# Attention with ScalarE's exponentials two units ahead, and the mLSTM state's decay on ScalarE: one core of a Trainium2

## What is computed

```python
s = jnp.einsum('bhtd,bhsd->bhts', qb, kb) * d_w
num = (jnp.einsum('bhts,bhse->bhte', s, vb)
       + inter_w[..., None] * jnp.einsum('bhtd,bhde->bhte', qb, c_mat))
...
h = num / jnp.maximum(jnp.abs(den), jnp.exp(-m_t))[..., None]
...
c_new = decay[..., None, None] * c_mat + jnp.einsum('bhsd,bhse->bhde', kb * w_s[..., None], vb)
```

```python
idx_score = jnp.where(admissible[None], idx_score.astype(jnp.float32), -jnp.inf)
_, sel = lax.top_k(idx_score, k_sel)
...
logits = jnp.einsum('bqgrd,bqkgd->bqgrk', qb, ks).astype(jnp.float32) * scale
p = jax.nn.softmax(logits, axis=-1).astype(v.dtype)
return jnp.einsum('bqgrk,bqkgd->bqgrd', p, vs)
```

## Time and profile before

| | |
|---|---|
| median of 3 runs | 2377.69 us (2368.26 to 2377.85) |
| the profiled execution, its own time | 2379.91 us |
| its span in the trace | 2377.9 us |
| mLSTM stage | 406.7 to 515.07 us |
| attention stage | 515.07 to 697.7 us |
| PE / DVE / ACT / POOL busy | 93% / 75% / 57% / 24% of the span |

### The profile page before, as it was taken

One profiled execution on the slowest core, in us unless ns is written; L12 is line 12 of the kernel. 1 busy time (PEld: TensorE's weight loads), 2 busy tenths in 40 slices (PEclk: granted clock), 3 DMA queues, 4 the chain that ended last, 5 costly groups with the idle time before them and its releaser, 6 DMA issues.

```text
span 2377.9 us, 41523 instructions
## 1 busy us (share of the span) xinstructions
PE 2202.8 (93%) x15519; PEld 1781.8 (75%) x15519; DVE 1793.9 (75%) x2040; ACT 1357.2 (57%) x1513; POOL 565.2 (24%) x466
## 2 busy tenths in 40 slices
PE   6899999859999579999999999999999999999994
PEld 5677887747887467787787787777777778778773
DVE  3699999933423578788788788788778877877886
ACT  4542224754643256666666666667667667667665
POOL 1017785863000011111111111111111211112110
PEclk8779999965999789999999999999999999999997
DMA  5011221020013268799899899899889889889897
GB/s 144 14 45 36 54 52 55 18 81 23 1 30 133 77 241 320 271 339 317 285 333 330 282 328 325 296 325 319 302 307 340 302 302 336 311 296 341 311 376 259
DMA packets 253533, 526.46 MB, mean 221 GB/s; under 512 B 32984, under 2 KB 59736, under 8 KB 253116
## 3 DMA queue, kind: packets, MB, share of 16 engines
q1 hardware_dynamic: 240204, 483.27, 56.5%
q0 software_dynamic: 13264, 42.34, 7.4%
HBM read 490.96 MB, written 35.91 MB: 222 GB/s over the span
## 4 chain that ended last, share of the span: by engine, by line
PE 70%; DMA 10%; DVE 7%; issue 4%; POOL 4%; ACT 3%; SPq 1%; DVEq 0%; ACTq 0%; POOLq 0%
PE ps L1757 13%; PE ps L1759 12%; PE ps L1758 12%; DMA e_raw<-in_w_gate_up_dram 9%; PE ps L1764 8%; PE ps L1425 5%; PE ps L1426 5%; PE ps L1427 5%; PE ps L1630 2%; PE ps L1640 2%; DVE e_wlo L2260 2%; PE ps L1580 2%; PE ps L1769 1%; PE ps L1500 1%; ACT a_p L1231 1%
## 5 line engine op out<-in xcount | busy, mean ns | idle before, releaser
L1308 ACT ACTIVATE e_whi<-e_raw 128x2048 fp32r<-128x2048 f32 x411 | 785.9, 1917 | 423.4 <-PE ps L1759 317.0
L2260 DVE TENSOR_TENSOR e_wlo<-e_raw,e_whi 128x2048 fp32r<-128x2048 f32 x410 | 926.9, 2285 | 68.8 <-ACT e_whi L1308 66.9
L1757 PE MATMUL ps<-e_whi,xh 128*128 128x512 f32 x1088 | 434.5, 399 | 0.0
L1758 PE MATMUL ps<-e_whi,xl 128*128 128x512 f32 x1088 | 424.3, 390 | 0.0
L1759 PE MATMUL ps<-e_wlo,xh 128*128 128x512 f32 x1088 | 424.1, 390 | 0.0
L941 POOL DMA_INDIRECT x_d<-ym,scur x34 | 69.6, 2048 | 867.3 <-ACT ym L1341 846.7
L1757 PEld LDWEIGHTS ps<-e_whi,xh 128*128 128x128 f32 x1088 | 204.2, 188 | 52.6 <-issue 12.7
L1759 PEld LDWEIGHTS ps<-e_wlo,xh 128*128 128x128 f32 x1088 | 204.2, 188 | 44.0
L1757 PE MATMUL ps<-e_whi,ath 128*128 128x512 f32 x544 | 222.3, 409 | 13.6 <-DVE atl L2288 13.6
L1758 PEld LDWEIGHTS ps<-e_whi,xl 128*128 128x128 f32 x1088 | 204.4, 188 | 39.3
L1759 PE MATMUL ps<-e_wlo,ath 128*128 128x512 f32 x544 | 213.8, 393 | 0.0
(11 more groups left out here) (353 smaller groups left out, 3404.1 us busy)
## 6 DMA issues: line engine op xcount, KB each, us to landing
e_raw<-in_w_gate_up_dram SPq DMA_DIRECT2D x275, 1024.0 KB, 6.5
e_raw<-in_w_down_dram SPq DMA_DIRECT2D x136, 1024.0 KB, 11.5
w_raw<-in_w_in_dram SPq DMA_DIRECT2D x20, 512.0 KB, 3.8
xt<-in_x_dram SPq DMA_DIRECT2D x8, 512.0 KB, 6.2
wo_raw<-in_w_out_dram SPq DMA_DIRECT2D x8, 512.0 KB, 7.4
xr<-in_x_dram SPq DMA_DIRECT2D x8, 512.0 KB, 4.2
x_d<-x SPq DMA_DIRECT2D x8, 512.0 KB, 2.6
h_d<-h SPq DMA_DIRECT2D x8, 512.0 KB, 2.9
```

The costliest lines, as they stand in the source:

```text
L1308: nc.scalar.activation(e_whi[:, m % HRING, :], e_raw[:, m % RING, :], ACT.Copy).then_inc(s.e_hi, 1)
L1757: nc.tensor.matmul(dst, a_hi, slot_hi, start=False, stop=False, skip_group_check=True)
L1758: nc.tensor.matmul(dst, a_lo, slot_hi, start=False, stop=False, skip_group_check=True)
L2260: nc.vector.tensor_tensor(e_wlo[:, m % HRING, :], e_raw[:, m % RING, :], e_whi[:, m % HRING, :].bitcast(F32), ALU.subtract).then_inc(s.e_l ...
```

## The change

ScalarE takes over the decay of the state: four ACTIVATE copies with a scale, from `state` to `state`, behind the four copies into `m_in` of the same chunk, with a new semaphore `a_dec`. GpSimd's four multiplications go; its sum now waits for `a_dec`. The waits for `p_in` and `g_st` go with them. In the attention, ScalarE runs `exp(0)` and `exp(1)` first and then, behind each copy `pt_out(u)`, `exp(u + 2)` in place of `exp(u + 1)`; `q_hi_of` and the other copies stand where they stood in the loop. PE's and VectorE's lists are the same, and so are all buffers.

```diff
+        self.a_dec = sem("a_dec")
...
             def m_state(c):
                 gp.wait_ge(s.a_up, c + 1)
-                gp.wait_ge(s.p_in, c + 1)
-                gp.wait_ge(s.g_st, c + 1)
-                for h in range(MH):
-                    m1(nc.gpsimd.tensor_scalar(state[:, h, :], state[:, h, :], decay[:, h, c:c + 1], 1.0, ALU.mult, ALU.mult))
-                m1.done()
+                gp.wait_ge(s.a_dec, c + 1)
                 nc.gpsimd.tensor_tensor(state[:], state[:], m_up[:], ALU.add).then_inc(s.g_st, 1)
...
                         m = nc.scalar.activation(m_in[:, h, :], ps[:, b, o_:o_ + MD + 1], ACT.Copy, scale=mexp[:, c, 0, h:h + 1])
                     m.then_inc(s.a_in, 1)
+                    for h in range(MH):
+                        m = nc.scalar.activation(state[:, h, :], state[:, h, :], ACT.Copy, scale=decay[:, h, c:c + 1])
+                    m.then_inc(s.a_dec, 1)
...
             exp(0)
+            exp(1)
             for u in range(NT * HEADS):
                 pt_out(u)
-                if u + 1 < NT * HEADS:
-                    exp(u + 1)
+                if u + 2 < NT * HEADS:
+                    exp(u + 2)
```

## The result

The changed kernel's median is 2349.82 us (4 runs, 2344.47 to 2350.25) beside 2373.75 for the kernel before on the same chip (2368.26 to 2377.85). The ratio is 0.9891, its 95% interval 0.9869 to 0.9913. It is not the quotient of the two medians and lies up to 0.2% from it.) That is faster, and by more than forecast: 24 us by the medians, and 29.6 us between the two profiled executions (spans of 2348.3 and 2377.9 us), where 18.8 was said. The median lies 0.8 us inside the range of 2349 to 2371, and outside the forecast's own range of 2354 to 2366. The profiled execution of before, 2379.91 us, took longer than each of the four runs above; that of the changed kernel did not stand out. So the traces show more of a difference than the medians do.

A forecast was written before the change was run, and what follows sets the result against it. The mLSTM loop was taken as bound by GpSimd, attention by PE with 17.0 us idle. Gains of 1.8 (loop), 2.4 (stage end) and 14.6 (attention) sum to 18.8 us, giving 2360 us, range 2349 to 2371 (own range 2354 to 2366).

The forecast's parts named there:

- The ring: mLSTM loop: the new chain of dependent steps from one m_w to the next takes 10.95 us against 11.25 a chunk.
- I add 0.4 for the split of the keys: End of mLSTM stage: 0.4 us for VectorE's key split meeting the last quotient, giving 8.9 us and a 2.4 us gain.
- the walk of the recorded waits: Attention: going through PE's recorded waits for unfinished exponentials, 14.8 us in 29 waits, led to a 14.6 us gain.
- 0.05 in each of 26: Attention: a matmul's record outlasts its turn, so each of 26 gaps is 0.05 us longer than recorded, 1.3 us.
- The upper bound is PE's whole idle time, 17.0: Attention: better order can win at most PE's idle time there, 17.0 us.
- In the sum it rises at the same unit.: Attention: the 18.8 us sum takes PE's clock to return to the upper level at the same unit, in block 3.
- Rival C: Attention: the clock rises earlier as PE has fewer gaps; 2354 us two pairs earlier, 2347 for a rise at 550; 12%.
- no rise in 20 gapless us, 550 to 570: Attention: argument against clock rivals C, that PE was busy all 20.00 us yet its clock stayed at 0.50.
- A: Attention: ScalarE holds PE elsewhere, the copy queued behind the later exponential and a mask; half the attention's gain, 2368 us; 12%.
- B: mLSTM loop: the ring exceeds 10.95 us because copies do not overlap; price 2 to 3 us, 2363 us; 10%.
- D: Attention: the clock rises later; 2.9 us per pair in block 3, up to 2395 us through block 5; 4%.
- E: Attention: PE's idle time only moves to the copy or masks and later stages absorb the rest; 2376 us; 4%.

The follow-up runs named there:

- e9: The changed kernel without the last mLSTM chunk's decay and sum into the state, which no chunk reads; 2345.37 us, ratio 0.9866 to the kernel before.
- e11: The changed kernel with 14 unread products in TensorE's idle stretches at the end of the mLSTM stage; 2347.27 us, ratio 0.9870 to the kernel before.
- e12: The changed kernel with the 14 unread products of e11 and without the last chunk's decay and sum; 2343.60 us, ratio 0.9865 to the kernel before.
- e1: The changed kernel with exponentials only one ahead, so only the decay moved; 2369.37 us, ratio 0.9977 to the kernel before.
- e6: The kernel before with two unread ScalarE copies ahead of the first exponential, starting attention about 2 us later; one execution, 2361.79 us.
- e15: The same kernel as e6, profiled again and timed in ten runs; 2373.8 us, ratio 1.0000 to the kernel before.
- e2: The kernel before with exponentials two ahead, the decay still on GpSimd; 2349.51 us, ratio 0.9909 to the kernel before.
- e13: e10 with 60 more small unread products in attention blocks 0 to 2; 2363.79 us, ratio 0.9960 to the kernel before.
- e14: e11 with 32 small unread products in attention block 0 and half of block 1; 2337.56 us, ratio 0.9868 to the kernel before.
- e10: The kernel before with 16 unread products in TensorE's idle stretches at the end of the mLSTM stage; 2371.19 us, ratio 0.9990 to the kernel before.
- e4: The kernel before, unchanged, profiled once more; one execution, 2379.0 us.
- e5: The changed kernel with two unread ScalarE copies ahead of the first exponential, starting attention some 2.2 us later; one execution, 2349.34 us.
- e8: The changed kernel with exponentials one ahead in attention blocks 0 and 1, two ahead from block 2 on; one execution, 2356.59 us.
- e3: The changed kernel, unchanged, profiled once more; one execution, 2344.43 us.
- e7: The changed kernel with exponentials two ahead only in attention blocks 0 and 1, one ahead from block 2 on; one execution, 2361.45 us.
- e17: The changed kernel with only the 32 small unread products of e14, none ahead of the first exponential; 2348.15 us, ratio 0.9883 to the kernel before.

## Why the prediction was right in direction and wrong on the clock

- **The mLSTM loop: right.** The ring of 10.95 us was measured as 10.92, the decay's copies were 1.28 us long in all, and GpSimd is idle 1.16 us a chunk for m_sc. 1.8 us was forecast, 1.95 found. This speaks for reading the copy's price from rows. By the Trainium skill's budget (ScalarE: Activation LUTs, Rules for kernel authors), added up copy by copy, the decay would have been an estimated 1.6 us and the loop slower. The trace does not agree, since the copies overlap and take 1.28 us.
- **The end of the mLSTM stage: right mechanism, wrong size.** 2.4 us was said, 1.33 measured, below the lower bound of 1.5. The step that failed is "I add 0.4 for the split of the keys". The first part of the last quotient took 2.59 us where in the loop it takes 1.09, 1.5 more, while VectorE worked on the splits. Its own lower bound ("if the quotient is slowed as the sum was") had the right cause. e9 took the useless sum and decay away and won 1.55 us there. Its trace also speaks for the splits as the cause: the quotient's first part took 1.09 us again, and the second, which now ran beside the splits (501.0 to 502.9), took 1.86 in place of 1.03:

```profile
500.11 1.09 POOL L839 TENSOR_SCALAR cols<-cols 128x1 f32<-128x1 f32 x4 [0.34 <-ACT cols L1215]
501.29 1.86 POOL L841 TENSOR_TENSOR cols<-cols 128x4 f32<-128x4 f32 x1
```

- **The attention at an equal clock: nearly right, a little small.** In blocks 4 to 7 the walk of the recorded waits gives 10.4 us, and 10.6 was measured. In blocks 0 to 3 it gives 4.2, and the runs show 6 to 6.6. The mis-sized term is "0.05 in each of 26", by which a record outlasts its turn; I had it from the upper clock. At the lower clock it is larger. From the first to the second transposes of a pair of block 2 PE took 553.50 - 551.43 = 2.07 us before, with no wait on record, and 547.39 - 545.52 = 1.87 after: 0.20 us was hidden in the busy time. PE's transposes, first before and then after, both at the lower clock:

```profile
551.43 0.90 PE L1630 MATMUL ps<-cst,a_p 128*128 128x128 f32 x3
...
553.50 0.90 PE L1630 MATMUL ps<-cst,a_p 128*128 128x128 f32 x3
```

```profile
545.52 0.90 PE L1631 MATMUL ps<-cst,a_p 128*128 128x128 f32 x3
...
547.39 0.85 PE L1631 MATMUL ps<-cst,a_p 128*128 128x128 f32 x3
```

  Over some ten pairs at that clock 0.15 more in each is 1.5 of the missing 2.3 us, an estimate; the other 0.8 is open. "The upper bound is PE's whole idle time, 17.0" was no safe bound either, for the same hidden gaps. The order is worth 10.6 + 6.5 = 17.1 us, an estimate that may be half a us too high.
- **The scores' wait in block 1: luck.** I had let it stand at 1.03 us; in the changed kernel it is 0.40, as VectorE's q_lo took 1.37 us in place of 2.42. The order did not do that. In other traces of the two-ahead order the wait was 1.73 us (e9), 1.70 (e11) and none (e12), and one ahead 1.49 (e1) and none (e6, e15). The q_lo ahead of it took 0.69 to 2.88 us, the longer the more of GpSimd's wo_lo (the low part of the output weights) ran beside it: 1.88 us of it in before, 0.46 in after, 2.15 in e9. VectorE's q_lo in before, then in e9:

```profile
533.78 2.42 DVE L2019 TENSOR_TENSOR q_lo<-qt,q_hi 128x512 fp32r<-128x512 f32 x1 [1.43 <-ACT q_hi L1160]
```

```profile
529.32 2.70 DVE L2022 TENSOR_TENSOR q_lo<-qt,q_hi 128x512 fp32r<-128x512 f32 x1 [1.42 <-ACT q_hi L1158]
```

- **The clock: this is the step that failed.** "In the sum it rises at the same unit." It rose at 551 in place of 583 (near 575 was expected of the changed kernel), some 11 of the 29.6 us between the two traces. Rival C had this case and its price (2347 for a rise at 550; the profiled execution took 2350.08), at 12%. Its chance was held down by one argument, "no rise in 20 gapless us, 550 to 570". That argument fails twice. The 20.00 us of busy time were not gapless: the pair above lies among them, and took 0.20 us longer than the same work at the same clock after the change. And e6 and e15, one kernel, had the rise 22 and 55 us behind exp(0): one execution's rise says little about the next. A moment that I had seen once was taken as a property of the order. By the medians the miss is smaller. The changed kernel won 23.9 us and e2 23.6, which is 3.5 and 6.5 more than their worth at an equal clock (20.4 and 17.1), so on average the clock gave some 3 to 6 us and not 11, an estimate.
- **What the rule of the clock gate was worth.** The Trainium skill (TensorE: Matmul & The Clock Gate, Part 1: The HAM clock gate) has sustained activity release the clock, and I set it aside. e13 and e14 agree with its direction: with the gaps filled, the clock stayed at 1.00 throughout. e11, 28 us with no gap on record and still at 0.50, does not agree with it, unless gaps too short for the records count.
- **Rivals A, B, D, E: not seen.** Transposes wait for a_t three times, 0.9 us in all. Scores do wait for masks, 2.7 us in five places. So PE was idle for 4.65 us in the attention, where 2 to 3 was named as the sign.

**What stays open.** Why the rise is where it is when PE is not kept busy. In the order before it came 22 to 68 us behind exp(0) in six traces (e6, e10, e15, e1, e4, before), in the two-ahead order 38 to 52 in seven, with a first short rise at +19 in one of them (e5). The two ranges overlap, so that the order brings the rise forward is likely and not shown. Gaps matter, since filling them held the clock; but e6 rose with gaps of 0.2 to 0.6 us in every pair and e11 stayed down without recorded ones. A rival that no run tests is the wait in block 1. Where it was 1.0 us or more (before, e1, e4, e8, e9, e11) the rise came at +41 to +68, and where it was under 0.8 (after, e2, e3, e5, e6, e7, e10, e12) at +22 to +46; only e15, with no wait and +55, stands against it. The runs of before spread over 7 to 14 us in each comparison, and e13's ten over 7.5. Part of that is not the attention's, as the rest of the program ran 1675 to 1681 us; that most of it is the clock's I take as likely, not as shown, since timed runs carry no trace. So the forecast's 18.8 us was near the worth of the change at an equal clock (1.95 + 1.33 + 17.1 = 20.4), and an earlier rise of the clock gave the rest.

## What to carry to other kernels

When a change fills gaps of TensorE in a stretch at the lower clock, give "the clock comes back earlier" more than a rival's chance, and price it from rows at either level. Read the clock's moment from several executions before building on it. Compare starts from unit to unit, not busy shares: a PE at 100% at the lower clock may still be waiting. If the stretch behind a stall is worth it, a few unread products in the stall and in the first gaps behind it can hold the clock. Both places were needed here, and 46 products won 12 us by the medians of two comparisons (2337.56 against 2349.82), with ratios of 0.9868 and 0.9891 whose intervals overlap; in the traces the attention went from 154.3 to 145.8 us. A single profile can be off the middle of the runs: the 29.6 us between two of them were 24 by the medians.

## What the runs showed of the hardware

- With the clock up, it was lost within 2.5 us of exp(0) although PE's idle stretches around it were of 0.4 to 1.3 us only (e10 to e12; in e11 0.82, 0.37 and 1.32 us between 507 and 512, and the fall at 512.4). Once down, it stayed down for 14 us (e17, 546.8 to 560.4) to 85 us (before, 498.0 to 583.3).
- One and the same kernel had the clock back 22 us behind exp(0) in one execution and 55 in another (e6, e15).
- Four ACTIVATE copies of 128x129 with a per-partition scale, SBUF to SBUF, take 1.28 us together (after, 497.51), like those of 128x128.
- Four GpSimd instructions on 128x1 columns took 2.59 us beside VectorE's splits (after) and 1.09 us otherwise (after's loop, e9). VectorE's split of 128x512 took 0.69 to 2.88 us in block 1, by what GpSimd did beside it (e6, e1).
